# Expert gate and up matrices loaded as two 64-partition transfers instead of one 128-partition transfer

## The reference

```
y = (silu(xb @ w_gate[e]) * (xb @ w_up[e])) @ w_down[e]      # w_gate[e], w_up[e]: 2048 x 512; w_down[e]: 512 x 2048
out[token] += weight * y
```

## Time and profile before

| | |
|---|---|
| median of three runs | 1197.78 us |
| profiled execution | 1198.11 us, span 1196.4 us |
| granted TensorE clock, mean | 0.86 |
| TensorE matmuls busy | 883.5 us (74%) |
| VectorE, ScalarE, GpSimd busy | 381.3, 231.6, 23.0 us |
| DMA | 460.93 MB in 47686 packets, mean 385 GB/s |
| HBM read, written | 458.05 MB, 2.36 MB |

### The profile page before, as it was taken

How to read it: one execution, slowest core, us unless ns; L and a number is a source line. 1 busy time by engine, 2 the same in 40 slices (tenths; PEclk the granted TensorE clock), 3 DMA queues, 4 the chain that set the end, 5 groups by cost and what they waited for, 6 DMA issues and landing times.

```text
span 1196.4 us, 17569 instructions
## 1 busy us (share of the span) xinstructions
PE 883.5 (74%) x7809; PEld 501.8 (42%) x7809; DVE 381.3 (32%) x493; ACT 231.6 (19%) x390; POOL 23.0 (2%) x66
## 2 busy tenths in 40 slices
PE   9999999999984666666666666666666666666666
PEld 7888888877431222222223232222222222222222
DVE  5454866545232222222222222222222222222233
ACT  6644655444200000000000000000000000000003
POOL 1200000000200000000000000000000000000000
PEclk9999999999997777778778787878787887878788
DMA  9875567878999999999999999999999999999997
GB/s 291 327 255 193 193 225 245 302 264 315 399 424 433 429 433 429 434 431 433 433 428 433 434 431 432 434 429 434 431 433 432 430 432 435 429 431 435 426 425 334
DMA packets 47686, 460.93 MB, mean 385 GB/s; under 512 B 4025, under 2 KB 4641, under 8 KB 32289
## 3 DMA queue, kind: packets, MB, share of 16 engines
q1 hardware_dynamic: 46704, 457.19, 92.4%
q0 software_dynamic: 864, 3.21, 0.8%
q10 hardware_dynamic: 80, 0.02, 0.0%
HBM read 458.05 MB, written 2.36 MB: 385 GB/s over the span
## 4 chain that ended last, share of the span: by engine, by line
DMA 50%; PE 47%; SPq 1%; ACT 1%; DVE 1%; issue 1%; POOLq 0%; DVEq 0%
DMA high_slots<-in_e_w_up 48%; PE scattered_out L1395 21%; PE bank L1605 12%; PE bank L1703 5%; PE pair L1566 3%; PE scattered_out L1716 1%; PE pair L1574 1%; DMA out_h<-acc 1%; ACT arena L780 1%; SPq L453 0%; DMA h<-in_x 0%; DVE acc L1261 0%; SPq L469 0%; PE pair L1582 0%; PE bank L1502 0%
## 5 line engine op out<-in xcount | busy, mean ns | idle before, releaser
L1199 DVE TENSOR_TENSOR acc<-scattered_out,acc 128x2048 f32<-128x2048 f32 x58 | 132.9, 2292 | 616.9 <-PE scattered_out L1716 616.9
L1605 PE MATMUL bank<-low_slots,arena 128*32 128x256 f32 x2048 | 153.5, 455 | 147.4 <-DMA low_slots<-in_e_w_up 147.0
L1605 PE MATMUL bank<-high_slots,arena 128*32 128x256 f32 x1952 | 146.0, 457 | 138.4 <-DMA high_slots<-in_e_w_up 138.4
L1605 PEld LDWEIGHTS bank<-low_slots,arena 128*32 128x32 f32 x2048 | 83.9, 126 | 218.8 <-issue 188.8
L1605 PEld LDWEIGHTS bank<-high_slots,arena 128*32 128x32 f32 x1952 | 79.6, 127 | 206.3 <-issue 178.7
L893 DVE TENSOR_TENSOR w_lo<-w_raw,w_hi 128x1024 fp32r<-128x1024 f32 x95 | 116.5, 1226 | 113.8 <-ACT w_hi L601 113.4
L601 ACT CAST w_hi<-w_raw 128x1024 fp32r<-128x1024 f32 x95 | 99.9, 1051 | 126.8 <-PE scattered_out L1395 120.7
L1395 PE MATMUL scattered_out<-w_hi,xT_second 128*128 128x512 f32 x376 | 121.4, 394 | 0.2 <-DVE w_lo L893 0.2
L1395 PE MATMUL scattered_out<-w_hi,xT_first 128*128 128x512 f32 x376 | 120.5, 393 | 0.1
L796 ACT COPY arena<-bank 128x256 f32<-128x256 f32 x32 | 11.9, 372 | 547.9 <-PE bank L1605 547.9
L1703 PE MATMUL bank<-down_slots,arena 128*32 128x512 f32 x944 | 107.9, 596 | 0.7 <-DVE arena L1193 0.7
(11 more groups left out here) (271 smaller groups left out, 512.1 us busy)
## 6 DMA issues: line engine op xcount, KB each, us to landing
down_slots<-in_e_w_down SPq DMA_DIRECT2D x26, 4096.0 KB, 21.1
low_slots<-in_e_w_gate SPq DMA_DIRECT2D x13, 4096.0 KB, 30.2
low_slots<-in_e_w_up SPq DMA_DIRECT2D x13, 4096.0 KB, 39.3
high_slots<-in_e_w_gate SPq DMA_DIRECT2D x13, 4096.0 KB, 30.5
high_slots<-in_e_w_up SPq DMA_DIRECT2D x13, 4096.0 KB, 39.7
w_raw<-in_a_w_in SPq DMA_DIRECT2D x64, 512.0 KB, 3.7
w_raw<-in_a_w_out SPq DMA_DIRECT2D x32, 512.0 KB, 5.0
down_slots<-in_e_w_down SPq DMA_DIRECT2D x6, 2048.0 KB, 19.4
```

The costliest lines, as they stand in the source:

```text
L1199: dve.tensor_tensor(acc[:, t, :], OUT[:, :], (acc if e else h)[:, t, :], ALU.add).then_inc(acc_done, 1)
L1605: ins = pe.matmul(GU[c * CAP:(c + 1) * CAP, 0:256], rows_k, gate_columns(rows_of[c // 2][k], c % 2), start=(a == 0 and k == 0), stop=(a == ...
```

## The change

Each gate and up matrix of experts 4 to 29 is now loaded by two transfers, issued one behind the other: the first for partitions 0 to 63, the second for partitions 64 to 127. Each partition still gets the same contiguous run of 32 KB. Both transfers add 16 to the semaphore of the matrix, so TensorE waits for 32 where it waited for 16. The down transfers and those of the other experts are as before.

```
             def load_wide(e, w):
-                sp.dma_start(wide_tile(e, w), (e_gate, e_up)[w][0, e].rearrange("(p k) n -> p k n", k=KD)
-                             ).then_inc(wide_in[e % 2][w], 16)
+                for p in (slice(0, P // 2), slice(P // 2, P)):
+                    sp.dma_start(wide_tile(e, w)[p, :, :], (e_gate, e_up)[w][0, e].rearrange("(p k) n -> p k n", k=KD)[p]
+                                 ).then_inc(wide_in[e % 2][w], 16)
...
                     for w in range(2 if a == 0 else 0):
-                        pe.wait_ge(wide_in[e % 2][w], 16 * m + 16 * ((e - LOOP) // 2 + 1))
+                        pe.wait_ge(wide_in[e % 2][w], 32 * m + 32 * ((e - LOOP) // 2 + 1))
```

## The result

The changed kernel takes 1905.58 us (median of 1900.34, 1905.58 and 1914.60), the kernel before 1197.67 us. The ratio is 1.592, with a 95% interval of 1.589 to 1.595: 708 us slower. The prediction said slower, 1700 us, with a range of 1400 to 1725. The direction is right; the size is 206 us short and outside the range.

What follows compares the result with a forecast made beforehand. The DMA engines, at a plateau of about 432 GB/s, were taken as the bound. Terms 0 + 0.5 + 0 + 505 = 505.5 us on 1198, with 3 us off for streams not in exact step, gave 1700 us; range 1400 to 1725.

Steps and rivals of the forecast that it cites:

- What bounds the kernel now: Wide experts: DMA engines are the bound, share 1.00 at 432 GB/s, 29.14 us per expert, whatever TensorE does.
- Steps 1 to 3: Gate and up loads: 52 more issues cost 0, 104 half transfers 0.5 us, TensorE's wait for 32 costs 0.
- Step 4: Writes into 64 partitions: half of 432 GB/s, 9.71 us a half transfer in place of 4.86, costing 505 us.
- no cost at all: Rival: each half of the partitions has its own 8 DMA engines, or engines are the limit; 1198.1 + 0.5 us; chance 0.16.
- TensorE and SP ... DMA stays the bound, and no second wait is added.: Wide rounds of 48.6 us: SP's next issue comes at least 19 us before queued matrices run out; nothing absorbed.
- All rounds are alike to 0.1 us: Wide rounds before the change: 39.35 and 38.91 us, taken as streams keeping very even pace, against drift.
- Out of step: Rival: streams sharing an entry write different halves, so halves cost less extra; 1210 to 1640 us, 1450 middle; chance 0.18.
- The exit: After the last up matrix: chunks unchanged, nothing absorbed; taken as 0, with 9 us for a lower clock in the range.

Runs made afterwards that it cites:

- the long stream: Loads only, the whole layer left out: six 4 MiB buffers, each loaded again once landed, six rounds a stage; lower and upper halves alone ran at 209 GB/s.
- v_sync: Against the changed kernel, SP also waits in each round from expert 6 on for that expert's gate and up to have landed; 1811.03 us.
- v_bsync: Against the kernel before the change, the same added SP wait in each round, for 16; 1262.44 us, ratio 1.053.

## Why the prediction was wrong

- *What bounds the kernel now.* Right, and shown by all kernels: their times follow the rate of the DMA engines in the wide stretch.
- *Steps 1 to 3 (more issues, cost per transfer, the wait for 32).* Predicted 0.5 us. Even and odd partitions measured them: ratio 1.0005, 0.7 us.
- *Step 4 (64 partitions take half the rate).* The mechanism is right: 419 GB/s for whole transfers and for even and odd ones, 206 for lower and upper. The size was a little low. I had taken exactly half of 432, 216 GB/s or 9.71 us a half; the long stream has 209 GB/s, 10.03 us, and so the term is 104 x (10.03 - 4.86) = 538 us in place of 505. In the kernel, with the engines in step, it measured 549 (v_sync against v_bsync) and 557 (the kernel with one wait against before; the wait itself and experts 4 and 5, which still run out of step, are in that number).
- *The rival "no cost at all"* fell: each half does not have DMA engines of its own.
- *"TensorE and SP ... DMA stays the bound, and no second wait is added."* This is the step that failed. It reckoned with 48.6 us of queued work that all 16 engines finish together. They don't. They are 2.2 us out of step before the first half transfer, with halves and wholes alternating the spread grows to 43 us by expert 10, and one engine ends up so late that the down transfer, which needs all 16, lands when the others have almost finished the gate and up transfers behind it. Since there is one down buffer, SP may issue the next group only after that. The wait which I excluded is in the trace (TensorE for down, 208.5 us from 420 to 1800), and the time from landing to issue, predicted at 17.8 to 29.5 us, is 1012.37 - 982.77 = 29.6 us in the round shown, of which 10.56 is this wait. One wait, which removes the offsets at expert 6, gives back 150 us.
- *"All rounds are alike to 0.1 us"*, from which the prediction took that the streams keep even pace, was misread. The two numbers behind it, 39.35 and 38.91, are 0.44 apart (the second does not stand in the earlier trace rows), and they run from SP's issue to a landing, which does not compare engines. The engines did keep pace before, but with a fixed spread of 3.7 us. The sum then counted being out of step as a gain of 3 us; the changed kernel loses about 150 us by it.
- *The rival "Out of step"* named the right quantity with the wrong sign. It argued that engines which share an entry hinder each other less when they are apart. For halves alone the runs show nothing of that in two long streams and something of it in one execution of the kernel with all matrices in halves. Where whole transfers come in between, the loss is what the runs show: 198 GB/s in place of 248.
- *The exit.* Predicted 0 to 9 us, measured 77.6 against 78.4 us: nothing.

The parts: 538 us for the rate of the halves as the long stream has it, 150 for the engines out of step and the others running dry behind them, together 688 of 708. The other 20 lie in the kernel with one wait, which is 557 above the kernel before; the wait and experts 4 and 5 are in that number, and I can't assign them further. The 150 can be split by an estimate from two stretches. From 411 to 1835 us the changed kernel has a share of 0.93 at 226 GB/s, and the kernel with one wait, from 512 to 1677, has 1.00 at 252. The missing 0.07 of 1424 us is about 100 us of dry engines, and the rest, some 50 us, is the lower rate of the engines that work (226 / 0.93 = 243 in place of 252). No run of the kernel has one of the two without the other. Nor is it shown which engines meet at which partitions, or which engine it is that falls behind.

## What to carry to other kernels

If a load must be cut by partitions, cut it so that each piece still spreads over all of them (every second partition, not the lower and the upper half): here that is the difference between no cost and 59%. A DMA share of 1.00 doesn't say that the engines move what they could; put the GB/s beside it. And where transfers of different partition patterns share a queue, look for stretches with a share of 0.06: one engine is then late, every semaphore waits for it, and a wait that lets all of them start together can pay for itself, as one did here with 150 us.

## What the runs showed of the hardware

- Transfers to partitions 0 to 63 or 64 to 127 move 200 to 210 GB/s, to 32 neighbouring ones 206, to 16 neighbouring ones 115, to every second partition 419 to 432, as whole ones do.
- A packet of 32 KB takes 1.21 us in a whole transfer and 2.5 us in a half one, and the DMA share is 0.97 to 1.00 in both.
- Two queues with a lower and an upper half transfer at the same time are no faster than one queue with both (1964 against 1906 us).
- In a stream of halves, halves, whole the lag of one DMA engine grows: in four rounds the spread went from 9.1 to 28 us, and from 2.7 to 19.5, and at the end only one or two engines were at work for 11 to 15 us. Where it began at 1.0 us it stayed under 2 for six rounds. In a stream of halves alone it stays what it is (10.5 and 8.6 us).
- Letting the queue run empty and filling it again costs 2.7 us ((1262.44 - 1198.26) / 24 rounds).
